# Projection results taken one step later, and values and keys turned one block round per step, in the two attentions of a streaming encoder layer

## The reference, cut to what matters

```python
xn = rmsnorm(h, g_pre_mix); y = xn @ w_in
q_a, k_a, v_a, f_a, q_b, k_b, v_b, g_a, g_b = split(y)
# FoX: 8 heads, causal, logits q.k/8 + sum of log f between key and query
p = softmax(q_a @ k_a.T * scale + bias);  o_fox = p @ v_a
# SWA: 8 query heads on 2 key heads, rotary, own chunk of 64 and two before, sinks
q_b, k_b = rope(q_b), rope(k_b);          o_swa = sink_softmax(...) @ v_b
mix = (sigmoid(g_a) * (o_fox @ w_o_fox) + sigmoid(g_b) * (o_swa @ w_o_swa)) @ w_out
```

## Time and profile before

| what | value |
|---|---|
| time, median of 3 runs | 1796.77 us (1795.99 to 1797.6) |
| the profiled execution | 1796.1 us |
| its span (first to last instruction) | 1794.2 us |
| PE busy in the span | 1731.9 us (97%) |
| DVE, ACT, POOL busy | 46%, 39%, 24% |
| PE clock granted | 0.998 of 2.4 GHz |

### The profile page before, as it was taken

How to read it: one execution, slowest core, us unless ns; L and a number is a source line. 1 busy time by engine, 2 the same in 40 slices (tenths; PEclk the granted TensorE clock), 3 DMA queues, 4 the chain that set the end, 5 groups by cost and what they waited for, 6 DMA issues and landing times.

```text
span 1794.2 us, 27881 instructions
## 1 busy us (share of the span) xinstructions
PE 1731.9 (97%) x10086; PEld 1604.1 (89%) x10086; DVE 833.2 (46%) x1911; ACT 705.3 (39%) x1421; POOL 437.3 (24%) x539
## 2 busy tenths in 40 slices
PE   4999999999999999989999999999999999999997
PEld 4999999999899999889988989899898989898995
DVE  5655556543899534454455423222232323232236
ACT  5277777765778433331333402122130303121121
POOL 1321111114333321144422312112130213121122
PEclk9999999999999999999999999999999999999999
DMA  5211211221222545554423302011020202011132
GB/s 174 61 51 44 74 55 56 82 83 49 62 69 58 172 159 187 171 168 132 167 94 106 106 12 71 25 47 47 23 70 17 65 12 70 23 47 47 36 141 106
DMA packets 136219, 145.24 MB, mean 81 GB/s; under 512 B 13032, under 2 KB 103464, under 8 KB 136128
## 3 DMA queue, kind: packets, MB, share of 16 engines
q1 hardware_dynamic: 136128, 144.06, 25.4%
HBM read 114.05 MB, written 28.19 MB: 79 GB/s over the span
## 4 chain that ended last, share of the span: by engine, by line
PE 59%; issue 3%; DMA 1%; DVE 1%; POOL 1%; ACT 0%; SPq 0%; POOLq 0%; ACTq 0%
PE gb L2401 23%; PE sc L2444 13%; PE tp L2444 6%; PE gb L430 5%; PE gb L2037 5%; PE tp L2196 2%; PE sc L2196 2%; PE tp L600 1%; POOL yacc L2504 1%; PE sc L1755 1%; DMA xr<-in_x_prompt 0%; DMA Ol<-o_scr 0%; PE po L1769 0%; DVE Ol L1990 0%; DMA hend<-h_scr 0%
## 5 line engine op out<-in xcount | busy, mean ns | idle before, releaser
L2401 PE MATMUL gb<-Mh,wh 128*128 128x384 f32 x768 | 259.8, 338 | 0.6 <-ACT osT_rl L2413 0.6
L2401 PE MATMUL gb<-Mh,wl 128*128 128x384 f32 x768 | 259.5, 338 | 0.0
L2401 PE MATMUL gb<-Ml,wh 128*128 128x384 f32 x768 | 259.4, 338 | 0.0
L2424 DVE TENSOR_TENSOR osT_rl<-osT_rl 128x384 f32<-128x384 f32 x96 | 83.4, 869 | 266.3 <-ACT osT_rl L2413 266.1
L416 POOL TENSOR_TENSOR wl<-raw,wh 128x256 fp32r<-128x256 f32 x172 | 135.0, 817 | 295.3 <-ACT wh L401 274.0
L718 PE MATMUL gb<-Xh,wh 128*128 128x384 f32 (+1 forms) x504 | 175.5, 348 | 0.0
L719 PE MATMUL gb<-Xh,wl 128*128 128x384 f32 (+1 forms) x504 | 170.7, 339 | 0.0
L720 PE MATMUL gb<-Xl,wh 128*128 128x384 f32 (+1 forms) x504 | 170.5, 338 | 0.0
L2388 POOL TENSOR_TENSOR dl<-raw,dh 128x1024 fp32r<-128x1024 f32 x32 | 76.8, 2400 | 340.5 <-ACT dh L2374 340.5
L2444 PE MATMUL sc<-dh,Ul 128*128 128x512 f32 x384 | 149.5, 389 | 0.0
L2444 PE MATMUL sc<-dl,Uh 128*128 128x512 f32 x384 | 149.5, 389 | 0.0
(11 more groups left out here) (337 smaller groups left out, 3942.4 us busy)
## 6 DMA issues: line engine op xcount, KB each, us to landing
raw<-in_w_in SPq DMA_DIRECT2D x70, 256.0 KB, 3.3
raw<-in_w_up SPq DMA_DIRECT2D x64, 256.0 KB, 3.6
raw<-in_w_down SPq DMA_DIRECT2D x64, 256.0 KB, 2.9
sig_scr<-sig SPq DMA_DIRECT2D x16, 576.0 KB, 3.1
kc<-in_cache_fox_k SPq DMA_DIRECT2D x8, 1024.0 KB, 5.7
vc<-in_cache_fox_v SPq DMA_DIRECT2D x8, 1024.0 KB, 7.5
sga<-sig_scr SPq DMA_DIRECT2D x8, 576.0 KB, 3.8
sgb<-sig_scr SPq DMA_DIRECT2D x8, 576.0 KB, 4.9
```

Of the source, the lines that this page charges most:

```text
L2401: last = nc.tensor.matmul(gb[c][:, 0:384], w_[j % 2][:, ws], x_[:, k, a:a + 384], start=(k == 0 and i == 0), stop=(k == KT - 1 and i == 2))
L2424: nc.vector.tensor_tensor(rl2, rl[m % 2], rl[m % 2], ALU.mult).then_inc(u_sq, 1)
```

## The change

- `V_STEPS` and `K_STEPS`: the value rounds go from t = 2, 2, 3 to t = 2, 3, 4, each behind three fills in place of two; the key rounds go from t = 5, 6, 7 to t = 6, 7, 8. The value store goes from t = 4 to 5, the key store from t = 9 to 10.
- A chunk that PE completes in step s is taken by ACT and DVE in step s+1, behind the turned P of that step (`ended(s)` is `FOX_ENDS[s-1]`), where most were taken at the end of step s. After the last step a loop takes the last chunk.
- The weights of FoX's units are rounded in two halves (`hi_half`), at the ends of steps s+1 and s+2 when a unit ends in s, where the whole was rounded at the end of s; `lo` goes two steps later.
- In SWA the takers go one step later: `swa_ended(s)` is `SWA_ENDS[s-1]`, for all three engines (ACT's, DVE's, and POOL's rotary part); the halves of the weights stay where they are.

```diff
+V_STEPS, K_STEPS = (2, 3, 4), (6, 7, 8)
@@ fox_pe
-                if p < 4 and t in (2, 3):
-                    for r in ((0, 1) if t == 2 else (2,)):
-                        m = min(at_ + 2, fill)
-                        fill_pe(pe, FOX_FILL, FOX_FILL_UNITS, s, at_, m)
-                        at_ = m
-                        v_round_pe(pe, p, r)
+                if p < 4 and t in V_STEPS:
+                    m = min(at_ + 3, fill)
+                    fill_pe(pe, FOX_FILL, FOX_FILL_UNITS, s, at_, m)
+                    at_ = m
+                    v_round_pe(pe, p, t - V_STEPS[0])
                 fill_pe(pe, FOX_FILL, FOX_FILL_UNITS, s, at_, fill)
-                if p < 4 and t in (5, 6, 7):
-                    k_round_pe(pe, p, t - 5)
+                if p < 4 and t in K_STEPS:
+                    k_round_pe(pe, p, t - K_STEPS[0])
+        def ended(s):
+            return FOX_ENDS[s - 1] if s >= 1 else []
@@ fox_act, behind fox_turned_act and ahead of fox_exp_act
-                for m, c in FOX_ENDS[s - 1] if s else ():
+                for m, c in ended(s):
                     if m == U_KB:
                         rope_act(act, Unit(m), c, c, 1.0)
+                    elif m in GATES:
+                        gate_act(act, Unit(m), c, GATES.index(m))
+                    elif m in (u_q(1), u_q(2), u_q(3)):
+                        q_keep(act, m, c, (m - 1) // 3)
...
-                for m, c in FOX_ENDS[s]:
-                    if m in GATES:
-                        gate_act(act, Unit(m), c, GATES.index(m))
-                    elif m in (u_q(1), u_q(2), u_q(3)):
-                        q_keep(act, m, c, (m - 1) // 3)
-                    if c == 2:
-                        if m == U_KB:
-                            rope_act(act, Unit(m), c, c, 1.0)
-                        hi(act, Unit(m + 2))
+                for x in range(2):
+                    for m, c in ended(s - x):
+                        if c == 2 and m < U_KB:
+                            hi_half(act, Unit(m + 2), x)
@@ fox_dve, behind fox_turned_dve
-                for m, c in FOX_ENDS[s - 1] if s else ():
+                for m, c in ended(s):
                     if m == U_KB:
                         rope_k_dve(v, c)
+                    elif m in (u_v(1), u_v(2), u_v(3)):
+                        v_keep(v, m, c, (m - 1) // 3)
+                    elif m in (u_k(1), u_k(2), u_k(3)):
+                        k_keep(v, m, c, (m - 1) // 3)
...
                 if s >= 4 and s % 2 == 0:
                     fox_out_dve(v, s // 2 - 2)
-                for m, c in FOX_ENDS[s]:
-                    if m == U_KB and c == 2:
-                        rope_k_dve(v, c)
-                    elif m in (u_v(1), u_v(2), u_v(3)):
-                        v_keep(v, m, c, (m - 1) // 3)
-                    elif m in (u_k(1), u_k(2), u_k(3)):
-                        k_keep(v, m, c, (m - 1) // 3)
@@ fox_pool
-                for m, c in FOX_ENDS[s]:
+                for m, c in ended(s - 1):
+                    if c == 2 and m < U_KB:
+                        lo(pool, Unit(m + 2))
...
@@ swa_act, behind qb_split_act; swa_dve alike; swa_pool
-                for m, c in SWA_ENDS[s]:
+                for m, c in swa_ended(s):
-                for m, c in SWA_ENDS[s - 2] if s >= 2 else ():
+                for m, c in SWA_ENDS[s - 3] if s >= 3 else ():
```

More of the change, by code:

```diff
@@ L135, in number_rounds @@
                 r += 1
-        if p < 4 and t in (2, 3):
[L137 to L141, removed]
-        if p < 4 and t in (5, 6, 7):
+        if p < 4 and t in V_STEPS:
+            V_ROUND.setdefault(p, []).append(r)
+            hi += 2
+            HI[r] = hi
+            r += 1
+        if p < 4 and t in K_STEPS:
             K_ROUND.setdefault(p, []).append(r)
@@ L1115, in fox_act @@
                         fox_turned_act(act, n, j)
-                for m, c in FOX_ENDS[s - 1] if s else ():
+                for m, c in ended(s):
                     if m == U_KB:
                         rope_act(act, Unit(m), c, c, 1.0)
+                    elif m in GATES:
+                        gate_act(act, Unit(m), c, GATES.index(m))
+                    elif m in (u_q(1), u_q(2), u_q(3)):
+                        q_keep(act, m, c, (m - 1) // 3)
                 if s < ITEMS:
                     fox_exp_act(act, s)
[L1121 to L1125, removed]
+                if p < 4 and t in V_STEPS:
+                    v_round_act(act, p, t - V_STEPS[0])
+                if p < 4 and t in K_STEPS:
+                    k_round_act(act, p, t - K_STEPS[0])
                 if s % 4 in (1, 2) and (s + 3) // 4 < 16:
@@ L1161, in fox_dve @@
                         fox_turned_dve(v, n, j)
-                for m, c in FOX_ENDS[s - 1] if s else ():
+                for m, c in ended(s):
                     if m == U_KB:
                         rope_k_dve(v, c)
-                if p < 4 and t in (2, 3):
-                    for r in ((0, 1) if t == 2 else (2,)):
-                        v_round_dve(v, p, r)
+                    elif m in (u_v(1), u_v(2), u_v(3)):
+                        v_keep(v, m, c, (m - 1) // 3)
+                    elif m in (u_k(1), u_k(2), u_k(3)):
+                        k_keep(v, m, c, (m - 1) // 3)
+                if p < 4 and t in V_STEPS:
+                    v_round_dve(v, p, t - V_STEPS[0])
                 if s % 4 == 2 and (s + 2) // 4 < 16:
@@ L1196, in fox_pool, with fox_keys_pool @@
                     fox_tail_pool(pool, s)
-                for m, c in FOX_ENDS[s]:
+                for m, c in ended(s - 1):
+                    if c == 2 and m < U_KB:
+                        lo(pool, Unit(m + 2))
+                for m, c in ended(s):
                     if m == U_KB:
[L1199 to L1204, removed]
+                        fox_keys_pool(pool, c)
+                if p < 3 and t == 7:
                     fox_keep_pool(pool, p + 1, u_q(p + 1), q_kept, qTs, nA[(p + 1) % 2], -1.0)
-                if p < 3 and t == 11:
+                if p < 3 and t == 12:
                     fox_keep_pool(pool, p + 1, u_k(p + 1), k_kept, kTs, nB, 1.0)
-                if p < 3 and t == 15:
-                    fox_keep_pool(pool, p + 1, u_v(p + 1), v_kept, vTs, nC, 1.0)
+                if 1 <= p < 4 and t == 1:
+                    fox_keep_pool(pool, p, u_v(p), v_kept, vTs, nC, 1.0)
+            for m, c in ended(STEPS):
+                fox_keys_pool(pool, c)
+                lo(pool, Unit(m + 2))
+        def fox_keys_pool(pool, c):
+            if c == 0:
+                pool.wait_ge(tab_in, 32)
+            rope_pool(pool, Unit(U_KB), c, c, kbT)
         def fox_sp(sp):
@@ L1544, in swa_pe, with swa_ended, swa_ended_act @@
             swa_values_pe(pe, GROUPS - 1)
+        def swa_ended(s):
+            return SWA_ENDS[s - 1] if s >= 1 else []
+        def swa_ended_act(act, s):
+            for m, c in swa_ended(s):
+                if m in GATES:
+                    gate_act(act, Unit(m), c, GATES.index(m))
+                else:
+                    u_ = (m - 17) // 2
+                    rope_copy_act(act, Unit(m), c, 3 + 3 * u_ + c, -SCALE)
         def swa_act(act):
```

20 lines of the change are left out of this document (11 added, 9 removed).

## The result

| | before | after |
|---|---|---|
| time, median of 7 runs each | 1795.99 us (1795.02 to 1797.6) | 1803.42 us (1800.31 to 1805.64) |
| the profiled execution | 1796.1 us | 1802.57 us |
| its span | 1794.2 us | 1800.8 us |
| PE, DVE, ACT, POOL busy (us) | 1731.9, 833.2, 705.3, 437.3 | 1734.7, 834.7, 705.0, 439.5 |
| PE clock granted | 0.998 | 0.996 |

The changed kernel is slower by 7.4 us: ratio 1.0038, interval [1.0029, 1.0048]. The forecast was 1799.8 us, some 3 us slower than before, with a range from 1791.5 to 1804.5.

A forecast was written before the change was run, and what follows sets the result against it. PE, busy for 97% of the span, was taken as the bound, so only its waits could be won. 1796.1 us + 0 (t = 2 to 7) + 3.0 (third rounds) + 0 (SWA), plus 0.7 to the median: 1799.8 us, range 1791.5 to 1804.5.

The forecast's parts named there:

- Values, t = 2 to 5: FoX's value rounds: the 0.75 us stall at 175.82 goes, later waits replace it; +0.8 us a phase.
- the clearing: DVE's clearing of `qs` (L862) behind a full value round: step 20's scores wait until 181.9, before 181.82.
- Item 19's second round: FoX, behind the small value round in step 20: PE waits for its bank, a new stall of 0.55 us.
- Keys: FoX, t = 6 to 8: second key round's stall at 194.98 goes, -0.8 us a phase; the one at 196.32 stays.
- Third rounds: FoX, t = 9 and t = 1: chunks delay the inverse, +0.44 and +0.56 us, three times each, +3.0 us in all.
- SWA: SWA's takers one step later: the same chain recurs one step later, 0 us, between -4 and +4.
- the forecast's own last sign: The forecast is wrong if SWA's scaling shows other than 3 to 6 us of PE's waits.
- Its other signs: Expected PE waits: longer for L862 and at t = 9, new at t = 1 and item 19, none at second key round.
- Rival 2: The clearing and SWA both get worse, rotary chunks' POOL instructions colliding with DVE's scaling: 1804 us; chance 0.15.
- Rival 1: The waits go and nothing follows, in FoX and SWA: 1788 us, or 1792 for half of it; chance 0.2.

The follow-up runs named there:

- clear_early: `swa_old` with DVE clearing `qs` ahead of the value round: 1794.03 us, ratio 0.9985 to the kernel before.
- values_only: The kernel before with only the value rounds and their store moved: 1798.85 us, ratio 1.0017.
- takers_only: `swa_old` with value and key rounds put back, leaving FoX's takers one step later and weights in halves: 1792.66 us, ratio 0.998 to the kernel before.
- swa_old: The changed kernel with SWA's takers put back as before, so only FoX changed: 1796.65 us against 1796.25 for the kernel before, ratio 1.0003.
- keeps_next: `swa_old` with DVE taking no chunk in steps t = 0 and 8 but in the next one: 1793.4 us, ratio 0.9986 to the kernel before.
- swa_only: The kernel before with only SWA's takers one step later: 1801.74 us, ratio 1.0028.
- both_fox: `swa_old` with `qs` cleared ahead of the value round and DVE's chunks kept out of t = 0 and 8: 1789.0 us, ratio 0.9957 to before.
- swa_gates: The kernel before with only SWA's gate chunks taken one step later: 1798.32 us, ratio 1.0013.
- swa_third: The kernel before with SWA's chunks taken only in every fourth step (s = 3, 7, ...): 1812.65 us, ratio 1.0082.
- best2: `both_fox` with PE turning the third value round behind one fill unit and key rounds one unit earlier: 1788.62 us, ratio 0.996 to the kernel before.

## Why the prediction came out as it did

**Values, t = 2 to 5: right in mechanism.** The stall at 175.82 went, the clearing became the next bound, and no wait stands behind L1053 ahead of t = 3. I had the clearing until 181.9 and it held PE until 182.23, since DVE's part waited for ACT's copies until 180.64, not 180.32. Item 19's second round, forecast at 0.55 us, lost 0.22: PE came later by the longer wait. `clear_early` shows that the two are one sum: without the first wait the second is 0.69. Per phase -0.75 + 1.04 + 0.22 = +0.5 us against +0.8 forecast, and `values_only` shows the part alone as a loss.

**Keys: right.** The stall at 194.98 went (-0.83), the one behind ACT's copy stayed (0.47, before 0.42). By `takers_only` it is not the move of the key rounds that removed it, for there they stand where they stood: it is the takers or the weights in halves. I had named both, the query chunk and the whole `hi`, and with them the key round, which was not needed.

**Third rounds: right in place and cause, too large in sum.** At t = 9 the loss grew from 0.78 to 1.03 us, and the second round added the 0.20 that I had called hidden; at t = 1 it grew from 0.22 to 0.66. By position PE fell behind 0.35 to 0.4 us a phase in all, where I had 1.0. Over values, keys and t = 9 the sum is 0.0, forecast +0.44: PE reached step 9 earlier. Some 0.2 us a phase of that are in no row with an idle time: before, the product of P and V of step 24 started 0.32 us behind a key round of two transposes (200.40 to 200.72), after it 0.35 us behind one of four (200.03 to 200.38), though two transposes take some 0.2 us less. At t = 1 it is 0.35 to 0.44, forecast 0.56. So FoX gave +0.4 us (`swa_old`; its stage +0.6) where the sum had +3.0: this term was too large by 2.6. `keeps_next` confirms the cause: without the chunks in those steps PTl's waits fall to 0.5 us.

**SWA: the term that failed.** "I take 0, between -4 (most of SWA's waits gone) and +4 us": `swa_only` measures +5.5 us, 3.8 of it as lost time in the stage. The argument was that the same chain recurs one step later. It does, but which step it falls in decides what it costs: five of nine chunks cost PE something before, eight after. I had the chunks' steps and PE's starts in the trace of before and did not lay one over the other. By the forecast's own last sign (it is wrong if SWA's scaling shows other than 3 to 6 us of waits) it fails: the list shows 6.7. Its other signs came: the wait for L862 over 1 us, none at the second key round, longer ones at t = 9 and, new, at t = 1. The wait behind L1053 ahead of item 19's second round is in no list, it is a loss of 0.2 us from start to start.

**Rival 2** named the right stage, and its 1804 us is the nearest number, but its mechanism did not come in that form. Scaling grew shorter in sum, not longer: seven are over 520 ns in `swa_only` where ten were before (the longest 1122 ns, 1103 in the earlier trace rows). Of L1385, eight are over 570 ns where three were, all beside a product of POOL. One such in `swa_only`, DVE and then POOL, beside L1385's usual 422 ns:

```profile
501.79 1.10 DVE L1385 TENSOR_TENSOR qs<-nA,qs 64x256 fp32r<-64x256 f32 x1
...
501.60 1.01 POOL L832 TENSOR_TENSOR u<-u,nC 128x384 f32<-128x384 f32 x1 [1.41 <-DMA u<-u]
```

L1385 has two inputs in SBUF. The Trainium skill (SBUF — State Buffer, "Who interferes with whom") has such an instruction contend with a GpSimd one that reads SBUF, besides the two-port modes that I had cited alone. The trace agrees. Counted over both lines it is +1.0 us of DVE's time, a quarter of the stage's 3.8 at most, for not all of DVE's time is PE's.

**The clock: not in the forecast.** Two stretches at half clock, 1.3 us each, are in the profiled execution's +6.5; the other 4 are 0.7 of FoX, 3.1 of SWA and 0.2 of what follows. Over the runs: `swa_only` took 1800.1 us in the median where 0.998 was granted (three runs) and 1802.7 at 0.996; the changed kernel's one run at 0.998 took 1800.31, its five at 0.996 1803.4. That suggests some 4 us of waits and 2 to 3 of clock, but does not show it: the groups are small, and the granted clock does not order every kernel's runs. The kernel before took 1796.2 us in the median at 0.998, 1795.8 at 0.997 and 1796.9 at 0.996, and `takers_only` 1792.4 at 0.998 and 1792.5 at 0.996.

**The number.** The measured 1803.42 lies in the range and 0.9 us above the forecast's own 1797.5 to 1802.5; as a difference it is +7.4 us where the forecast had +3.0. The direction was forecast from FoX's term, and the loss lies mostly in SWA. That the total lies in the range at all is luck: a FoX term too large by 2.6 us stood in for a part of an SWA term too small by 5.5; the SWA error alone would have brought the forecast to 1805.3, outside the range. Rival 1 had 1788 us, and `both_fox` gives 1789; but that is another kernel, with the two chains taken out and SWA as before, so it shows what the moves can win in FoX and not that rival 1 was right.

## What to carry to other kernels

When work moves from one step of a pipeline to the next, lay its steps over the bottleneck engine's slack step by step; "the same chain one step later" is not the same cost. Moving an instruction by a step helps only if nothing else stands in the place it moves to: here a full round ahead of a clearing, and a chunk ahead of an inverse, took back all that the move had won, and putting these two elsewhere turned +0.4 us into -7.4. Distance on the producer's engine was worth nothing while the reader's order was fixed. And where a change has a stage to itself, the marks of PE at the stage's ends tell a cost of 1 us from one profile, if the unchanged stages agree; here FoX's did within 0.2 us and SWA's did not.

## What the hardware showed that I had not expected

A wait of PE of 1.3 to 1.5 us is followed by a stretch at half clock in some executions and at some places, and not at others: the same wait for L862 stands four times in the changed kernel, and only behind the one at 259.70 did the clock fall (from 1.00 to 0.50); in `values_only` it was the one at 182.68, and in `swa_old` and `keeps_next` none of the four. The wait of some 1.4 us at SWA's start stands in all 14 profiles; a stretch of half clock follows it in five of them (after, `swa_gates`, `swa_third`, `takers_only`, `best2`). Each costs 1.2 to 1.3 us, nearly as much as the wait itself. In `swa_third`, with waits of 4.4 and 4.8 us, four such stretches came, and its runs spread from 1809.8 us at 0.996 to 1815.8 at 0.992. What decides whether the clock falls was not tried.
